# Attention phases of a two-block model on one core: scores, transposes and the latent norm placed elsewhere in the engines' queues

## The chip, the core and the metric

One core of a Trainium2 chip (trn2) runs the whole program in one launch. The metric is the device time of that launch in microseconds, lower is better. Engines are named as in the profile: PE (TensorE), DVE (VectorE), ACT (ScalarE), POOL (GpSimd) and SP (SyncE), which issues the weight loads.

## The reference, cut to what matters

Two blocks run on 256 tokens of width 2048 in fp32: first an even and an odd layer, then a retention layer with an MLP. The change lies in the odd layer:

```python
h = rms_norm(x, norm_w); proj = h @ w_in
c_q, c_kv, k_r, z_c, mq, mz = _split(proj, ODD_SPLITS)        # 768, 512, 64, 2048, 512, 512
q  = (rms_norm(c_q,  mla_q_norm_w)  @ mla_w_uq ).reshape(b_, l_, 16, 128 + 64)
kv = (rms_norm(c_kv, mla_kv_norm_w) @ mla_w_ukv).reshape(b_, l_, 16, 128 + 128)
q_nope, q_rope = q[..., :128], rope(q[..., 128:], positions)
k_nope, v = kv[..., :128], kv[..., 128:]
k_rope = broadcast(rope(k_r[:, :, None, :], positions))       # one rotated key for all heads
y_c = causal_block_attention([q_nope, q_rope], [k_nope, k_rope], v) * silu(z_c)
y_m = memory_attention(mq, mem_n, w_mk, w_mv) * silu(mz)      # 4 heads of 128, 256 memory rows
return x + concatenate([y_c, y_m]) @ w_out
```

## The kernel before, in words

**Panels.** All weight products run as a stream of panels in the order of the table PHASES. A panel is a column of 128 outputs with 4 to 16 weight tiles of 128x128. SP loads it into raw (four slots). ACT rounds it to fp32r (w_hi, L405), DVE takes the rest (w_lo, L744); both are done two panels ahead and in two halves, by the helper split(name, i, j, h) of each engine. PE multiplies each tile twice (L1461: w_hi by the high and low parts, 512 columns; L1464: w_lo by the high part, 256 columns). Two accumulators (pj) alternate: when a panel is done, ACT copies one half of the sum (copy_half, L410), DVE adds the other (evac, L753, or L756 and L758 where it is scaled), and only then may the panel after the next begin. Every engine runs its own queue in order, written out by hand. Semaphores tie them together, so an instruction that waits holds all behind it on its engine.

In ACT's and DVE's queues, split(j, 0) waits until PE has begun the second half of panel j (its buffers are two panels deep), split(j, 1) follows the evacuation of panel j.

**The phases around the change.** "latent" and "latent_tail" (11 panels of 16 tiles) give the latents lraw (4 tiles for c_kv, 6 for c_q) and the shared key krA. Behind them ACT squares all ten tiles at once (L615), PE sums the squares over the partitions with ten matmuls against ones (L1704), ACT takes exp(-0.5 ln v) twice (rsqrt, L414 to L418), DVE refines by a Newton step (L769 to L775), rotates krA (L988 to L1194), and scales and splits the latents into lat (L1199, L1207, hi_lo at L763 and L765).

"memq" (L622, L1212, L1707) runs twice over four panels of 16 tiles: two query heads, two gate columns. After panel 2 PE makes the scores of two heads (L1599), after panel 3 it transposes the probabilities (L1478) and multiplies by the values (L1611). DVE scales one latent tile per panel (normalise_q), and takes softmax_shift and softmax_scale together before it splits and evacuates panel 3. At the end of each pass the gate is applied (L1225, L1228, hi_lo), which counts y_mem.

"mla" (L642, L1238, L1724) runs eight times over eight panels with 6, 6, 6, 8, 4, 4, 16 and 16 tiles: q of two heads, the two heads' rope parts, k of two heads (panel 3 has two outputs of 4 tiles), v of two heads, two gate columns. POOL turns the rope part of q (L376) once panel 2 is evacuated, DVE finishes the rotation (L1266, L1268) in its step for panel 3, between split(3, 0) and split(3, 1). PE makes the scores after panel 4 (L1738, L1739), transposes the values after panels 5 and 6 and the probabilities after panel 6 (L1478), and multiplies them after panel 7 (L1758, L1760).

**POOL's queue.** Between the phases POOL issues a few transfers. After y_mem 8, the end of memq, come the mask (L368) and the first half of x from x_spill (L369); it then waits until x has landed (L370) and only then enters the mla loop with L376:

```python
            pool.wait_ge(S["y_mem"], 8)
            pool.dma_start(mask, mla_mask).then_inc(S["mask_loaded"], 16)
            pool.dma_start(xflat[:, 0:2048], x_spill[:, 0:2048]).then_inc(S["x_loaded"], 16)
            pool.wait_ge(S["x_loaded"], 48)
            ...
                pool.wait_ge(evacuated, outputs("mla", i)(2, 1 + NB))
```

DVE waits for the mask (L1235) ahead of the mla loop.

Of the kernel before, what the change touches and what calls it, by code (L numbers as in the profile page):

```python
# [26 lines left out]
T = 256  # L27
# [4 lines left out]
F32 = mybir.dt.float32  # L32
# [78 lines left out]
def build(nc, streams, w_dt, vecs, consts, mla_mask, ret_tab, ret_decay, pos, x, mem, out):  # L111
    ctx = ExitStack()
    with ctx:
# [80 lines left out]
        def cut(j, n):  # L194
# [21 lines left out]
            angle_ready sin_ready mask_loaded latent_ready latent_squares lat_ready krope_ready  # L216
# [127 lines left out]
        def _(pool):  # L344
# [21 lines left out]
            pool.wait_ge(S["x_spilled"], 32)  # L366
            pool.wait_ge(S["y_mem"], 8)
# [25 lines left out]
        def _(act):  # L393
# [225 lines left out]
            rsqrt(NORM["kv"] + 1, *norm_kv[0:2])  # L619
            rsqrt(NORM["q"] + 1, *norm_q[0:2])  # L620

            def memq_body(i):  # L622
                O = outputs("memq", i)
                M = Count(4, 2, i)
                for j in range(4):
                    if j == 3:
                        mem_exp(M, 2, lambda u: mx[:, u], [p_m[:, 0:512], p_m[:, 512:1024]],
                                [vh_m[:, 0:256], vh_m[:, 256:512]],
                                lambda u: values[:, :, bass.ds(i * 256 + 128 * u, 128)])
                    split("memq", i, j, 0)  # L630
                    copy_half("memq", i, j)
                    if j < 3:
                        split("memq", i, j, 1)
                act.wait_ge(evacuated, O(3, 1 + NB))
                A(mt_m, mz_m, ACT.Tanh, scale=0.5).then_inc(S["mz_tanh"], 1)
                for u in range(2):
                    act.wait_ge(S["mem_pt"], M(u, 1))
                    A(pt_m[:, 512 * u:512 * u + 512], mx[:, 2 + u], ACT.Copy).then_inc(S["mem_pt_copied"], 1)
                split("memq", i, 3, 1)
            act.wait_ge(S["kv_loaded"], 16)  # L640
            run(act, "memq", memq_body)
            def mla_body(i):  # L642
                O = outputs("mla", i)
                for j in range(8):
                    if j == 6:
# [7 lines left out]
                        act.drain().then_inc(S["mla_probs"], 1)  # L653
                    if j == 7:
# [5 lines left out]
                    if j != 3:  # L660
                        split("mla", i, j, 0)
# [72 lines left out]
        def _(dve):  # L734
# [253 lines left out]
            def rope(dst, tmp):  # L988

                for h in range(4):  # L990
                    a, b = 32 * h, 32 * (h ^ 1)
                    TT(tmp[a:a + 32], dst[b:b + 32], sinT[b:b + 32], ALU.mult)
                dve.drain()
                TT(dst, dst, cosT, ALU.mult)
                dve.drain()
                ins = TT(dst, dst, tmp, ALU.add)
                dve.drain()
                return ins

# [187 lines left out]
            variance(NORM["kv"] + 1, 0, 512, norm_kv[0])  # L1187
            variance(NORM["q"] + 1, 1, 768, norm_q[0])

            dve.drain()  # L1190
            rope(krA, rope_t)
            v.tensor_copy(krB[64:128], krA[64:128])
            v.memset(krB[0:64], 0.0)
            dve.drain()  # L1194
            v.memset(krA[64:128], 0.0).then_inc(S["krope_ready"], 1)
            dve.wait_ge(S["rsqrt_ready"], NORM["kv"] + 1)
            newton(*norm_kv)
            for c in range(4):
                STT(out=lraw[:, c], in0=lraw[:, c], scalar=V("kv_norm", c), in1=norm_kv[3], op0=ALU.mult,  # L1199
                    op1=ALU.mult)  # L1200
            hi_lo((lat[:, 0:4, 0], lat[:, 0:4, 1]), lraw[:, 0:4]).then_inc(S["lat_ready"], 1)
            dve.wait_ge(S["rsqrt_ready"], NORM["q"] + 1)
            newton(*norm_q)

            def normalise_q(c):
# [775 lines left out]
```

## Time and profile before

| | |
|---|---|
| median of 3 runs | 2830.67 us (2828.84 to 2835.06) |
| profiled execution | 2829.0 us, its span 2827.5 us |
| PE busy | 2759.5 us, 98% |
| DVE busy | 1956.2 us, 69% |
| ACT busy | 1412.8 us, 50% |
| POOL busy | 35.4 us, 1% |
| L744 (w_lo) | 1010 times, mean 1130 ns |
| L405 (w_hi) | 1010 times, mean 978 ns |
| L1461 / L1464 (hs) | 4400 times each, mean 400 / 280 ns |

All times are on the profile's clock from the start of the span. Matmuls overlap: an L1461 and an L1464 of 400 and 280 ns follow each other so that a pair starts every 0.35 us. memq begins at about 888 us and mla at 960 us; mla ends at about 1208 us.

### The profile page before, as it was taken

The page shows a single profiled execution, that of the slowest core. Times are in us where ns is not written, and L with a number is a line of the kernel's source. Part 1 is how long each engine was busy: PE and PEld are TensorE (multiplying, and loading weights), DVE is VectorE, ACT ScalarE, POOL GpSimd, SP SyncE. Part 2 cuts the span into 40 slices and gives each one's busy share as a digit, 9 for nine tenths or more (in the row PEclk, how much of TensorE's full clock was granted, in tenths as well). Part 3 has the DMA queues.
Part 4 walks back from the last instruction along what each step waited for, and adds up shares of the span by engine and source line. Part 5 has one row for each costly group of instructions (what it writes and reads, how often), then busy time and mean ns, then how long its engine had stood idle before and what let it go on. Part 6 is the DMA issues. An engine that isn't in the chain of part 4 may idle for free.

```text
span 2827.5 us, 46051 instructions
## 1 busy us (share of the span) xinstructions
PE 2759.5 (98%) x15758; PEld 2394.6 (85%) x15758; DVE 1956.2 (69%) x3098; ACT 1412.8 (50%) x2218; POOL 35.4 (1%) x56
## 2 busy tenths in 40 slices
PE   6999999999999899999999999999999999999998
PEld 5888888888888788888888888888888888888887
DVE  5566568878777677777766666666777576675775
ACT  5544345555554555556555544555554444444444
POOL 0000000000000001000000000000000000000000
PEclk9999899999999999999999999999999999999999
DMA  5555354444674334466545555555555555555553
GB/s 231 196 186 185 119 194 157 157 146 144 213 241 162 105 128 159 152 189 200 181 169 177 179 191 186 172 175 171 174 190 185 187 185 187 185 187 185 186 186 112
DMA packets 76349, 495.73 MB, mean 175 GB/s; under 512 B 8544, under 2 KB 8672, under 8 KB 23792
## 3 DMA queue, kind: packets, MB, share of 16 engines
q1 hardware_dynamic: 73568, 478.18, 49.3%
q0 software_dynamic: 2000, 13.70, 1.3%
q10 hardware_dynamic: 704, 2.83, 0.3%
q8 instruction: 47, 0.77, 0.1%
q14 instruction: 30, 0.25, 0.0%
HBM read 486.29 MB, written 8.39 MB: 175 GB/s over the span
## 4 chain that ended last, share of the span: by engine, by line
PE 92%; DVE 3%; ACT 2%; DVEq 2%; issue 1%; DMA 1%; ACTq 0%; POOLq 0%
PE pj L1461 56%; PE pj L1464 28%; PE mx L1478 1%; PE mx L1534 1%; ACT w_hi L405 1%; DVE w_lo L744 1%; PE pj L1570 1%; PE mx L1798 0%; PE mx L1805 0%; DVEq L947 0%; PE mx L1623 0%; PE mx L1738 0%; PE mx L1739 0%; PE mx L1790 0%; PE mx L1611 0%
## 5 line engine op out<-in xcount | busy, mean ns | idle before, releaser
L1461 PE MATMUL pj<-hs,w_hi 128*128 128x512 f32 x4400 | 1564.5, 400 | 4.8 <-DVE xT L758 4.8
L744 DVE TENSOR_TENSOR w_lo<-raw,w_hi 128x1024 fp32r<-128x1024 f32 x1010 | 1136.7, 1130 | 469.3 <-ACT w_hi L405 451.2
L405 ACT ACTIVATE w_hi<-raw 128x1024 fp32r<-128x1024 f32 x1010 | 982.6, 978 | 652.7 <-PE pj L1461 640.2
L1464 PE MATMUL pj<-hs,w_lo 128*128 128x256 f32 x4400 | 1230.1, 280 | 0.0
L1461 PEld LDWEIGHTS pj<-hs,w_hi 128*128 128x128 f32 x4400 | 827.0, 188 | 202.3 <-DVE xT L758 5.1
L1461 PE MATMUL pj<-ys,w_hi 128*128 128x512 f32 x2496 | 885.7, 400 | 8.5 <-DVE ys L809 4.0
L1464 PEld LDWEIGHTS pj<-hs,w_lo 128*128 128x128 f32 x4400 | 830.6, 189 | 3.6 <-issue 2.9
L1464 PE MATMUL pj<-ys,w_lo 128*128 128x256 f32 x2496 | 700.6, 281 | 0.0
L1461 PEld LDWEIGHTS pj<-ys,w_hi 128*128 128x128 f32 x2496 | 471.1, 189 | 126.2 <-DVE ys L809 4.3
L1464 PEld LDWEIGHTS pj<-ys,w_lo 128*128 128x128 f32 x2496 | 473.2, 190 | 0.0
L410 ACT ACTIVATE half<-pj 128x256 f32<-128x256 f32 x491 | 186.6, 380 | 571.8 <-PE pj L1464 559.5
L753 DVE TENSOR_TENSOR gen<-pj,half 128x256 f32<-128x256 f32 x412 | 173.8, 422 | 148.1 <-ACT half L410 146.3
L1461 PE MATMUL pj<-lat,w_hi 128*128 128x512 f32 x272 | 102.3, 415 | 3.9 <-DVE gen L753 2.4
L949 DVE TENSOR_TENSOR xT<-xT,gen 128x256 f32 (+1 forms) x144 | 61.3, 425 | 27.9 <-issue 27.5
L1464 PE MATMUL pj<-lat,w_lo 128*128 128x256 f32 x272 | 76.9, 283 | 0.0
L1461 PEld LDWEIGHTS pj<-lat,w_hi 128*128 128x128 f32 x272 | 51.8, 190 | 20.8 <-issue 4.9
L523 ACT ACTIVATE gen<-xT 128x256 f32 (+1 forms) x64 | 26.8, 418 | 63.6 <-DVE xT L949 63.4
L1464 PEld LDWEIGHTS pj<-lat,w_lo 128*128 128x128 f32 x272 | 52.1, 192 | 0.2
L765 DVE TENSOR_TENSOR ys<-gen,ys 128x256 f32 (+2 forms) x84 | 37.8, 450 | 13.6 <-issue 13.3
L756 DVE TENSOR_TENSOR gen<-pj,half 128x256 f32<-128x256 f32 x59 | 25.0, 423 | 26.2 <-ACT half L410 25.9
L1478 PE MATMUL mx<-con,xT 128*128 128x128 f32 x136 | 21.2, 307 | 20.7 <-DVE xT L802 19.3
L954 DVE TENSOR_TENSOR gen<-gen 128x256 f32<-128x256 f32 x80 | 32.3, 420 | 11.8 <-ACT gen L523 11.8
(279 smaller groups left out, 1411.9 us busy)
## 6 DMA issues: line engine op xcount, KB each, us to landing
raw<-in_w_up SPq DMA_DIRECT2D x64, 1024.0 KB, 4.7
raw<-in_w_down SPq DMA_DIRECT2D x64, 1024.0 KB, 4.8
raw<-in_w_ssd SPq DMA_DIRECT2D x48, 1024.0 KB, 4.7
raw<-in_w_ret_a SPq DMA_DIRECT2D x48, 1024.0 KB, 4.7
raw<-in_w_ret_b SPq DMA_DIRECT2D x48, 1024.0 KB, 4.8
raw<-in_w_out SPq DMA_DIRECT2D x64, 640.0 KB, 3.9
raw<-in_w_gate SPq DMA_DIRECT2D x32, 1024.0 KB, 4.8
raw<-in_w_mem SPq DMA_DIRECT2D x16, 1024.0 KB, 4.9
```

The costliest lines, as they stand in the source:

```text
L405: A(w_hi[:, s, 0:b - a, :], raw[:, c.slot(p, 4), a:b, :], ACT.Copy).then_inc(hi_ready, 1)
L410: A(half[:, c.slot(o, NB)], pj[:, c.slot(o, NB), 0:T], ACT.Copy).then_inc(half_copied, weight)
L744: TT(w_lo[:, s, 0:b - a, :], raw[:, c.slot(p, 4), a:b, :], w_hi[:, s, 0:b - a, :].bitcast(F32), ALU.subtract).then_inc(split_ready, 1)
L753: TT(dst, pj[:, k, T:2 * T], half[:, k], ALU.add).then_inc(evacuated, weight)
L765: return TT(dst[1], src, dst[0].bitcast(F32), ALU.subtract)
L949: TT(xo, xo, res[(o + u) % 2], ALU.add).then_inc(S["x_tile"], 1)
L954: TT(acc[k], acc[k], sq[k][o % 2], ALU.add)
L1461: ins = mm(pj[:, k], w_hi[:, s + h, u], m, start=opens and t == 0, stop=False)
L1464: ins = mm(pj[:, k, 0:T], w_lo[:, s + h, u], m[:, 0], start=False, stop=closes and t == order[-1])
L1478: return nc.tensor.transpose(dst, src, ident)
L1534: ins = mm(mx[:, 0, 32 * r:32 * r + 32], hs[:, k, part, 128 * r:128 * r + 128].bitcast(F32), wdt[:, k], start=k == 0 and part == 0, stop=k ...
L1570: ins = mm(pj[:, k], w_hi[:, s + h, u], src[:, t], start=t == 0, stop=False)
```

## The change

Five edits. PE sums squares over only two tiles (one per norm), after DVE has added the ten tiles to two; these two matmuls stand in the middle of memq's first panel. The memory scores and the transposes of the probabilities move into panels 2 and 3 of memq. memq is written out twice, and the latent scaling is cut in pieces: ACT makes the high part, DVE the low part. The key's rotation goes from DVE to POOL, and the second memory gate goes behind panel 2 of the first mla pass. In mla the scores go from behind panel 4 into panel 6 (before its tile 2), the value transposes into panel 6 (tile 10), the probability transposes into panel 7 (tile 9). DVE and ACT handle the softmax one panel later and after the split of the same step. The mask is waited for in panel 6's step.

```diff
 @@ POOL
             pool.wait_ge(S["x_spilled"], 32)
+            pool.wait_ge(S["krope_in"], 1)
+            for h in range(4):
+                a, b = 32 * h, 32 * (h ^ 1)
+                nc.gpsimd.tensor_tensor(rope_t[a:a + 32], krA[b:b + 32], sinT[b:b + 32], ALU.mult)
+            pool.drain()
+            nc.gpsimd.tensor_tensor(krA, krA, cosT, ALU.mult)
+            pool.drain()
+            nc.gpsimd.tensor_tensor(krA, krA, rope_t, ALU.add)
+            nc.gpsimd.memset(krB[0:64], 0.0)
+            pool.drain()
+            nc.gpsimd.tensor_copy(krB[64:128], krA[64:128])
+            pool.drain()
+            nc.gpsimd.memset(krA[64:128], 0.0).then_inc(S["krope_ready"], 1)
             pool.wait_ge(S["y_mem"], 8)
 @@ ACT, memq (and, per pass, latent_high pieces: wait lat_scaled k, copy to lat[:, c, 0])
-            rsqrt(NORM["kv"] + 1, *norm_kv[0:2])
-            rsqrt(NORM["q"] + 1, *norm_q[0:2])
...
                 for j in range(4):
-                    if j == 3:
+                    split("memq", i, j, 0)
+                    if i == 0 and j == 0:
+                        rsqrt(NORM["kv"] + 1, *norm_kv[0:2])
+                        rsqrt(NORM["q"] + 1, *norm_q[0:2])
+                    if i == 0 and j == 1:
+                        latent_high(1, 4)
+                    if j == 2:
                         mem_exp(...)
...
                     copy_half("memq", i, j)
...
+                    split("memq", i, j, 1)
 @@ ACT, mla
+                for j in range(8):
+                    if j != 3:
+                        split("mla", i, j, 0)
+                    if j == 6:
+                        exps()
                     if j == 7:
                         act.wait_ge(S["mla_vt"], i * 1 + 1)
...
-                    if j != 3:
-                        split("mla", i, j, 0)
 @@ DVE, latent_tail
                 split("latent_tail", 0, j, 0)
+                if j == 2:
+                    dve.wait_ge(S["latent_squares"], 1)
+                    TT(lsq[:, 0:2], lsq[:, 0:2], lsq[:, 2:4], ALU.add)
+                    TT(lsq[:, 4:7], lsq[:, 4:7], lsq[:, 7:10], ALU.add)
+                    dve.drain()
+                    TT(lsq[:, 0], lsq[:, 0], lsq[:, 1], ALU.add)
+                    TT(lsq[:, 4], lsq[:, 4], lsq[:, 5], ALU.add)
+                    dve.drain()
+                    TT(lsq[:, 4], lsq[:, 4], lsq[:, 6], ALU.add).then_inc(S["latent_sums"], 1)
                 evac("latent_tail", 0, j, ...)
                 split("latent_tail", 0, j, 1)
...
-            rope(krA, rope_t)
...
+            dve.drain().then_inc(S["krope_in"], 1)
 @@ DVE, memq (low_latent(k, c): wait lat_hi k, subtract into lat[:, c, 1])
                 for j in range(4):
-                    if j < 3:
-                        normalise_q(i * 3 + (4 + j))
-                    if j == 3:
+                    if j == 2:
                         softmax_shift(M, 2, lambda u: mx[:, u])
+                    split("memq", i, j, 0)
+                    if i == 0 and j == 0:
+                        variance(NORM["kv"] + 1, 0, 512, norm_kv[0])
+                        variance(NORM["q"] + 1, 1, 768, norm_q[0])
+                    if i == 0 and j == 2:
+                        dve.wait_ge(S["krope_ready"], 1)
+                    if j == 2:
                         softmax_scale(M, 2, [p_m[:, 0:512], p_m[:, 512:1024]])
...
                     evac("memq", i, j, ...)
...
+                    split("memq", i, j, 1)
+                    if i == 0 and j == 0:
+                        dve.wait_ge(S["rsqrt_ready"], NORM["q"] + 1)
+                        newton(*norm_q)
+                        newton(*norm_kv[0:3], lnv)
+                        scale_latent(4, "q_norm", lrstd).then_inc(S["lat_scaled"], 1)
...
+                if i == 0:
+                    memq_gate(0)
-            run(dve, "memq", memq_body)
-            dve.wait_ge(S["mask_loaded"], 16)
+            memq_body(0)
+            memq_body(1)
 @@ DVE, mla
-            def mla_body(i):
+            def mla_body(i, opening=False):
                 for j in range(8):
-                    if j == 5:
+                    if j == 6:
+                        dve.wait_ge(S["mask_loaded"], 16)
                         dve.wait_ge(S["mla_scores"], i * 1 + 1)
...
+                    if j != 3:
+                        split("mla", i, j, 0)
                     if j == 6:
                         dve.wait_ge(S["mla_probs"], i * 1 + 1)
...
-                    if j != 3:
-                        split("mla", i, j, 0)
...
                     split("mla", i, j, 1)
+                    if opening and j == 2:
+                        memq_gate(1)
...
-            run(dve, "mla", mla_body)
+            mla_body(0, True)
+            run(dve, "mla", mla_body, 1)
 @@ PE
-            pe.wait_ge(S["latent_squares"], 1)
...
+            def latent_stats():
+                pe.wait_ge(S["latent_sums"], 1)
+                for k, c in ((0, 0), (1, 4)):
+                    mm(mx[:, k, 0:T], ones, lsq[:, c], start=True, stop=True).then_inc(S["stat_ready"], 1)
...
+                def scores():
+                    pe.wait_ge(evacuated, O(1, 1 + NB))
...
+                def probs():
...
+                    whole("memq", i, j, hs,
+                          mid={8: latent_stats} if i == 0 and j == 0 else {5: scores} if j == 2 else
+                          {10: probs} if j == 3 else {})
...
                     panel("mla", i, j, (
...
+                        mid={2: scores, 10: value_rows} if j == 6 else {9: probs} if j == 7 else {})
```

In the diff, `mid={t: f}` runs f on PE's queue before tile t of that panel.

## Rows read from the trace of the kernel before

**Rows 1.** PE's waits over the whole span: who was waited for, total us, times, longest

```profile
PE mx L1738 <- DVEq L1269: 9.2, 8, 1.3
PE mx L1611 <- ACT xT L638: 4.9, 2, 2.5
PE pj L1461 <- DVE xT L758: 4.8, 1, 4.8
...
PE pj L1461 <- DVE gen L753: 3.5, 7, 2.4
```

**Rows 2.** Timeline of PE around the squares' sums: start us, length us, line

```profile
888.39 4.58 PE L1704 MATMUL mx<-xT,con 128*128 128x256 f32 x20
...
908.84 0.80 PE L1461 MATMUL pj<-hs,w_hi 128*128 128x512 f32 x1 [4.77 <-DVE xT L758]
```

**Rows 3.** Stretches: us, PE, PEld, DVE, ACT, POOL busy (instructions), granted clock, DMA

```profile
913.00:914.00 1.00, 1.00 (x6) 0.84 (x5) 1.00 (x2) 0.00 (x0) 0.00 (x0) 0.83 0.95 401
...
968.00:969.00 1.00, 1.00 (x5) 0.80 (x4) 0.76 (x2) 0.99 (x3) 0.00 (x0) 0.50 1.14 418
```

**Rows 4.** Timeline of PE, first value product, first mla panel and its panel 6

```profile
927.36 3.49 PE L1611 MATMUL mx<-xT 128*128 128x256 f32 x8 [2.37 <-ACT xT L638]
...
960.08 0.58 PE L1461 MATMUL pj<-lat,w_hi 128*128 128x512 f32 x1
...
980.18 0.48 PE L1461 MATMUL pj<-hs,w_hi 128*128 128x512 f32 x1
```

**Rows 5.** Timeline of ACT, the two rsqrt

```profile
893.35 0.42 ACT L418 ACTIVATE xT<-xT 128x256 f32<-128x256 f32 x1
893.79 1.28 ACT L414 ACT_TABLE_LOAD   x1
...
896.01 1.28 ACT L405 ACT_TABLE_LOAD   x1
```

**Rows 6.** Timeline of DVE, the split behind the squares and one Newton step

```profile
889.31 1.23 DVE L744 TENSOR_TENSOR w_lo<-raw,w_hi 128x1024 fp32r<-128x1024 f32 x1 [3.45 <-ACT w_hi L405]
...
897.41 0.42 DVE L769 TENSOR_TENSOR xT<-xT 128x256 f32<-128x256 f32 x1
...
899.42 1.67 DVE L1199 SCALAR_TENSOR_TENSOR gen<-gen,vec,xT 128x256 f32<-128x256 f32 x4
```

**Rows 7.** Timeline of DVE, the second memory gate

```profile
960.47 0.69 DVE L1228 SCALAR_TENSOR_TENSOR xT<-mx,xT 128x512 f32<-128x512 f32 x1 [1.85 <-PE mx L1611]
...
961.92 0.69 DVE L765 TENSOR_TENSOR ys<-xT,ys 128x512 f32 x1 [0.17 <-issue]
```

**Rows 8.** Timeline of POOL, the load of x and the first rotation

```profile
963.71 0.53 POOL L369 DMA_DIRECT2D xT<-x_spill  x1
971.45 3.21 POOL L376 TENSOR_TENSOR gen<-gen 32x256 f32<-32x256 f32 x4 [7.21 <-DVE gen L753]
```

**Rows 9.** DMA issues from 955 to 1010 us: KB each, median us to landing

```profile
xT<-x_spill POOLq DMA_DIRECT2D x1, 1024.0 KB, 5.9
```

**Rows 10.** Timeline of PE in the second mla pass, panel 4 to panel 6

```profile
1004.83 0.28 PE L1464 MATMUL pj<-lat,w_lo 128*128 128x256 f32 x1
1006.40 0.49 PE L1738 MATMUL mx<-gen 128*128 128x128 f32 x2 [1.29 <-DVEq L1269]
...
1009.47 0.40 PE L1461 MATMUL pj<-lat,w_hi 128*128 128x512 f32 x1
...
1010.67 0.48 PE L1461 MATMUL pj<-hs,w_hi 128*128 128x512 f32 x1
```

**Rows 11.** Timeline of DVE in the same pass

```profile
1004.52 0.96 DVE L744 TENSOR_TENSOR w_lo<-raw,w_hi 128x256 fp32r<-128x256 f32 x1
...
1006.52 1.56 DVE L744 TENSOR_TENSOR w_lo<-raw,w_hi 128x256 fp32r<-128x256 f32 x2 [0.20 <-issue]
1008.00 0.42 DVE L753 TENSOR_TENSOR gen<-pj,half 128x256 f32<-128x256 f32 x1
...
1014.61 1.01 DVE L1257 TENSOR_SCALAR xT<-xT,small 128x128 f32<-128x128 f32 x4
```

More of the change, by code:

```diff
@@ L629, in memq_body, with exps @@
                                 lambda u: values[:, :, bass.ds(i * 256 + 128 * u, 128)])
-                    split("memq", i, j, 0)
+                    if j == 3:
+                        for u in range(2):
+                            act.wait_ge(S["mem_pt"], M(u, 1))
+                            A(pt_m[:, 512 * u:512 * u + 512], mx[:, 2 + u], ACT.Copy).then_inc(S["mem_pt_copied"], 1)
                     copy_half("memq", i, j)
-                    if j < 3:
[L633 to L639, printed above, removed]
+                    if j == 3:
+                        act.wait_ge(evacuated, O(3, 1 + NB))
+                        A(mt_m, mz_m, ACT.Tanh, scale=0.5).then_inc(S["mz_tanh"], 1)
+                    split("memq", i, j, 1)
+                    if i == 0 and j == 2:
+                        latent_high(2, 5)
+                        latent_high(3, 6)
+                    if i == 0 and j == 3:
+                        latent_high(4, 7)
+                    if i == 1 and j == 0:
+                        latent_high(5, 8)
+                        latent_high(6, 9)
+                    if i == 1 and j == 2:
+                        latent_high(7, 0, 4)
             act.wait_ge(S["kv_loaded"], 16)
-            run(act, "memq", memq_body)
+            memq_body(0)
+            memq_body(1)
             def mla_body(i):
                 O = outputs("mla", i)
-                for j in range(8):
-                    if j == 6:
+                def exps():
                         act.wait_ge(S["mla_shift"], i * 1 + 1)
@@ L1196, in _ @@
[L1196 to L1205, printed above, removed]
-                STT(out=lraw[:, c], in0=lraw[:, c], scalar=vec[:, bass.ds(c + VEC["kv_norm"][0], 1)],
-                    in1=lrstd, op0=ALU.mult, op1=ALU.mult)
-                yy = lat[:, c]
-                hi_lo((yy[:, 0], yy[:, 1]), lraw[:, c]).then_inc(S["lat_ready"], 1)
+            dve.drain().then_inc(S["krope_in"], 1)
@@ new lines, in memq_body @@
+                    if i == 0 and j == 3:
+                        low_latent(2, 5)
+                        low_latent(3, 6)
+                        scale_latent(7, "q_norm", lrstd).then_inc(S["lat_scaled"], 1)
+                    if i == 1 and j == 0:
+                        low_latent(4, 7)
+                    if i == 1 and j == 1:
+                        low_latent(5, 8)
+                        low_latent(6, 9)
+                    if i == 1 and j == 3:
+                        low_latent(7, 0, 4)
@@ new lines, in memq_body @@
+                    if i == 1 and j == 0:
+                        for c in (8, 9):
+                            scale_latent(c, "q_norm", lrstd).then_inc(S["lat_scaled"], 1)
+                    if i == 1 and j == 1:
+                        for c in range(4):
+                            ins = scale_latent(c, "kv_norm", lnv)
+                        ins.then_inc(S["lat_scaled"], 1)
+                if i == 0:
+                    memq_gate(0)
+            memq_body(0)
+            memq_body(1)
```

122 lines of the change are left out of this document (54 added, 68 removed).

## The prediction

> **What bounds it now.** I began with the page: PE is busy 98% of the span, so a gain can only be a wait of PE, a matmul left out, or a stretch at the lower clock. The second view is the list of PE's waits. In these phases they are few: 9.2 us before the mla scores, once in each of the 8 passes, 4.9 before the memory values (two), 4.8 before memq's panel 2 and, within the 3.5 of the last row, one of 2.4 before mla's panel 2, where DVE sits out the mask's load [rows 1]. The third view is PE's timeline: the ten matmuls on the squares are 20 instructions in 4.58 us, 0.23 each, and nothing runs beside them [rows 2]. The fourth is the granted clock: behind a long wait it falls to 0.50, which is 1.2 GHz: the tile at 908.84 takes 0.80 us instead of 0.40 [rows 2], the clock is back at 2.4 GHz from about 913.4, and it is 0.50 again at 968 [rows 3]. The first value product took 3.49 us for 8 instructions, where 8 times 0.23 is 1.83 [rows 2, 4]; so such a stretch costs about 1.7 us, and the one behind the wait of 4.77 us, from 908.8 to 913.4, about 2.3 (half of 4.6). The fifth view is DVE's timeline inside an mla pass, because DVE releases every panel.
>
> **Part 1, squares.** 16 of the 20 instructions go: -3.7 us [rows 2]. The two left wait for DVE's sums. DVE issues the split at 889.3 and is free 1.14 us later, at 890.45 [rows 6]; the adds follow: 0.69 and about 0.95 for 512 and 768 columns, three of 0.42 and the drains (0.42 for 256 columns, 0.69 for 512 [rows 6, 7]; 768 extrapolated), 2.9 in all: 893.35. PE reaches tile 8 of memq's panel 0 at about 891.0. A wait of 2.4 us is new; before it was 0.25.
>
> **Part 2, memq's norm chain.** PE goes on at 893.4, spends 0.9, is at tile 8 at 894.3 and ends panel 0 at 897.1 (8 tiles of 0.35). ACT's split for panel 2 needs that tile 8, and both rsqrt now stand behind it: split 894.8 to 895.9, table load 1.28, Ln and Exp, load, Ln and Exp, a third load [rows 5]: about 902.05. Only then comes copy_half of panel 0, and DVE's evacuation at 903.3. Panel 2 needs it: PE is done with panel 1 at 902.65 and waits 0.7. Then DVE has in one row: split 1.14, two Newton steps of 2.0 [rows 6], a scaling 0.5, split 1.14, and the evacuation of panel 1, 0.85: 903.5 + 7.6 = 911.1. PE wants that one before tile 5 of panel 2, for the scores, at 905.1: a wait of 6.0. So the 4.8 of [rows 1] does not go; the chain of tables and Newton steps is as long as before and takes its place. In memq's second pass the gate of the first, two splits and five small operations on DVE make a wait of 1.6 at the same tile. The transposes inside panel 3 do remove the two waits before the values: six tiles (2.1 us) now cover ACT's copies. Waits in memq: before 0.25 + 4.8 + 4.9 = 10.0; after 2.4 + 0.7 + 6.0 + 1.6 = 10.7. Clock: before 2.3 + 1.7, after 2.3. Sum of parts 1 and 2: -3.7 + 0.7 - 1.7 = **-4.7**; mla begins at 955.4 instead of 960.1 [rows 4].
>
> **The key's rotation on POOL** is free for PE if it ends before DVE's softmax_scale, over 15 us later. The nearest price is 3.21 us for four operations on 32 partitions [rows 8]: seven to ten such, and by partitions up to 14 us. Its harm is to DVE: beside POOL's rotation a split of 256 columns took 0.96 us, where the two in [rows 11] share 1.56 with one of four times the size. I take 0 and keep 0 to 2 us. The Trainium skill, SBUF — State Buffer, section "Who interferes with whom", says that a DVE instruction with two SBUF inputs and a GpSimd one that reads SBUF lock each other out for a whole instruction; by that rule the split ahead of the variances is held by one POOL operation and the sum gains 0.8.
>
> **Part 3, first mla pass.** This is the dear one. The second gate moves behind panel 2. It ends in y_mem 8, and behind y_mem 8 in POOL's queue stand the mask, the load of x, the wait until x has landed, and only then the rotation of q. Count from M, the pass's first tile. Panels 0 to 2 (18 tiles of 0.353) end at M+6.4; DVE splits, evacuates panel 2 at 7.7, splits until 8.1. The gate is an operation of 0.77, then 2.14 from L1228 to the end of L765 [rows 7]: M+11.0. POOL issues the load of x 1.1 later (962.61 to 963.71, [rows 7, 8]), it lands 5.9 after issue [rows 9]: M+18.0. Rotation 3.2 [rows 8], DVE's part 0.9 and gap, then the split that panel 5's second half waits for: M+22.9. Split of panel 6 (1.14) and evacuation of panel 4 (0.4): panel 6 begins at M+24.5. Its 34 tiles ahead are 12.0, so 12.5 us are waits, 2.2 of them before panel 4 (its output waits behind the gate) and 9.5 inside panel 5. Behind 9.5 us without work the clock is low as in [rows 3]: I take 1.6. Before, panel 6 came at M+20.1 [rows 4]: 12.0 for tiles, 2.9 for scores and transposes, 5.1 waits and clock. Pass 1: 12.5 + 1.6 - 5.1 = **+9.0**. The mask's own wait of 2.4, in that 5.1, is hidden now; the load of x is not.
>
> **Part 4, the seven other passes.** The scores leave the place between panels 4 and 5, and with them the 1.29 us wait for DVE's L1269. But they were the cover for DVE. Its order up to the second split of panel 6 is unchanged: the first split of panel 5 ends at 1005.48, the rotation follows, the second split of panel 5 ends at 1006.93, that of panel 6 at 1008.08, and the evacuation of panel 4, which panel 6 must have, at 1008.42 [rows 11]. PE is done with panel 4 at 1004.95. Now it waits 0.6 for the first, works 0.7, waits 0.8 for the second, works 0.7, waits 0.8 for the third: panel 6 begins at 1008.47. Before it began at 1010.67 [rows 10], with 2.72 for scores (1006.40 to 1009.47 less a tile) and 0.22 for two transposes ahead of it, which move behind. 1008.47 + 2.94 - 1010.67 = +0.74 a pass, times seven: **+5.2**. Behind that nothing waits: scores end 3.4 after panel 6's start, the softmax needed 6.5 from 1009.1 to 1015.6 [rows 11], is put behind a split on either engine (1.3), and is wanted 8.4 after the scores; the copies for the value product keep about 0.6 us of cover. If that cover is gone, each pass pays what is missing, up to the 1.1 us of one ACT split.
>
> **Sum.** -4.7 + 9.0 + 5.2 = +9.5 us on the profiled 2829.0, that is 2838.5. The median of the runs is 1.7 higher, and I give the time on its basis: **2840.2**. Bounds of the parts: 1 and 2 from -8 (no third table load, a shorter chain) to -1 (POOL in DVE's way, a low clock behind the 2.4 us wait too); 3 from +5 (x lands in 3 us, clock holds) to +11; 4 from +4 to +9. The likeliest case's own range is 2835 to 2846. 0.2% is 5.7 us and about what a measurement of this kernel can tell from no change; so 2825.0 and 2836.3 are the borders.
>
> **Rivals.**
> Waits gone (faster, 0.12): the mla scores come out of DVE's way and panels 5 and 6 find their weights ready. It would need DVE's steps at 1006.5 and 1008.0 to come earlier; they depend on the evacuations of panels 3 and 4 and on POOL, which the change leaves. The place is panel 6's start; it decides if DVE is ready within 1.1 us of panel 4's end, not 3.5. Each pass then saves 1.3 to 1.45, 10 for seven; with -4.7 and +9.0, 2824.8. Against it speak [rows 11].
> Load of x hidden (0.20): POOL's wait ends early, because x lands sooner or the gate comes sooner, and pass 1 costs 0 to +2. Then -4.7 + 1 + 5.2: 2832. For it: a mean of 5.9 for a single transfer is one sample; against it, even a load of 2.6 us would leave 6 of waits.
> Clock falls in the loop (0.10): in 3.5 us after panel 4 PE works only 1.4, in seven passes. Each fall costs 1.7, so +12 on the sum: 2852. Against it: behind the wait of 1.29 us the tiles take 0.40 us, the length at full clock [rows 10]. The Trainium skill, TensorE: Matmul & The Clock Gate, section "A second HAM failure mode: psum-queue depth-cycling", says that short idles between groups can make the clock swing; no row here shows it for gaps this short.
> Nothing moves (0.03): the edit acts only where PE was idle anyway; 2830.7.
> Forecast, parts as worked: 0.55.
>
> **Chances.** Slower by over 0.2%: 0.50 of the forecast's 0.55, the clock's 0.10, a little of the load's: 0.62. Within 0.2%: 0.26. Faster: 0.12. The range 2827 to 2850 leaves out the fast rival, and the clock rival's far end.
>
> **What the profile of after should show.** PE's waits: the row for the mla scores gone; in its place about 0.6, 0.8 and 0.8 us at L1461 in panels 5 and 6, eight times, released by DVE's L744 and L753; an mla pass 0.7 to 0.8 us longer. In pass 1 a single wait near 9.5 us inside panel 5 and POOL's L376 (its new line) beginning about 7 us behind DVE's last step of the gate. In memq a wait of 6 us before the scores, no wait before the values, four instructions on the squares instead of 20. If mla passes are shorter than before, part 4 is wrong; if mla's pass 1 is not at least 5 us longer, part 3 is; if memq's first scores do not wait, part 2.

## The result, and the profile after

The changed kernel takes 2836.88 us (median of 20 runs, 2828.88 to 2840.64), the kernel before on the same chips 2828.71 (20 runs, 2822.80 to 2835.06): a ratio of 1.003, 95% interval 1.0023 to 1.0038, so 8.2 us slower. Forecast were 2840.2 and slower; the range 2827 to 2850 holds it. The profiled execution took 2840.31 us, its span 2838.8.

**PE's waits**, the whole span: engine, line waited for, total us, times, longest.

```profile
PE pj L1514 <- DVE w_lo L778: 16.1, 16, 9.1
PE pj L1514 <- DVE gen L787: 6.9, 15, 1.5
PE mx L1652 <- DVE xT L792: 5.9, 2, 5.0
...
PE mx L1758 <- DVE xT L1215: 2.1, 1, 2.1
```

The row for the mla scores [rows 1] is gone, and so is the one for the memory values. In their place stand DVE's splits (L778) with 16.1 us, of which 9.1 are a single wait, and its evacuations (L787). The timeline of PE shows where:

```profile
894.21 2.05 PE L1758 MATMUL mx<-xT,con 128*128 128x256 f32 x4 [2.06 <-DVE xT L1215]
...
912.11 3.78 PE L1652 MATMUL mx<-kv,xT 128*128 128x256 f32 x8 [5.02 <-DVE xT L792]
...
942.92 1.99 PE L1652 MATMUL mx<-kv,xT 128*128 128x256 f32 x8 [0.87 <-DVE xT L792]
...
956.53 0.58 PE L1514 MATMUL pj<-lat,w_hi 128*128 128x512 f32 x1
...
967.66 0.50 PE L1514 MATMUL pj<-lat,w_hi 128*128 128x512 f32 x1 [1.49 <-DVE gen L787]
...
979.17 0.79 PE L1514 MATMUL pj<-lat,w_hi 128*128 128x512 f32 x1 [9.12 <-DVE w_lo L778]
...
1009.89 0.49 PE L1514 MATMUL pj<-lat,w_hi 128*128 128x512 f32 x1 [0.42 <-DVE w_lo L778]
1011.28 0.49 PE L1514 MATMUL pj<-lat,w_hi 128*128 128x512 f32 x1 [0.43 <-DVE w_lo L778]
1012.75 0.50 PE L1514 MATMUL pj<-hs,w_hi 128*128 128x512 f32 x1 [0.51 <-DVE gen L787]
```

In this order they are: the four instructions of the sums; the memory scores of both passes; mla's first tile; in pass 1 panel 4 and the second half of panel 5; in pass 2 the three small waits, in panel 5 (twice) and at panel 6, that come back in each later pass.

**Why the 9.1.** DVE's and POOL's timelines in pass 1:

```profile
966.58 0.69 DVE L799 TENSOR_TENSOR ys<-xT,ys 128x512 fp32r<-128x512 f32 x1
...
977.64 0.42 DVE L1316 TENSOR_TENSOR gen<-gen 128x256 f32<-128x256 f32 x1 [9.37 <-POOL gen L389]
```

```profile
967.57 0.60 POOL L381 DMA_DIRECT2D xT<-in_mla_mask  x1 [63.73 <-DVE ys L799]
968.17 0.54 POOL L382 DMA_DIRECT2D xT<-x_spill  x1
974.57 3.04 POOL L389 TENSOR_TENSOR gen<-gen 32x256 f32<-32x256 f32 x4 [5.86 <-DMA xT<-x_spill]
```

The gate ends at 967.3, POOL issues mask and x, waits 5.86 us for x and turns q only then. DVE stands for 9.37 us with the split of panel 5 queued behind the wait.

**The granted clock** in stretches (us, PE, PEld, DVE, ACT, POOL busy, clock, DMA):

```profile
894.00:900.00 6.00, 5.79 (x23) 4.94 (x24) 4.07 (x7) 2.37 (x3) 3.60 (x4) 0.72 0.46 153
...
912.00:914.00 2.00, 1.89 (x5) 1.53 (x6) 2.00 (x5) 0.00 (x0) 0.00 (x0) 0.50 0.00 0
914.00:916.00 2.00, 2.00 (x6) 1.64 (x5) 1.16 (x4) 0.00 (x0) 0.00 (x0) 0.50 0.84 221
916.00:918.00 2.00, 2.00 (x7) 1.65 (x7) 0.79 (x2) 0.00 (x0) 0.00 (x0) 0.51 0.72 303
...
1338.00:1341.00 3.00, 3.00 (x11) 2.52 (x11) 0.84 (x3) 0.41 (x2) 0.00 (x0) 0.50 0.22 90
```

The clock is at 1.2 GHz behind the wait of 2.06 us (until about 897.5), behind that of 5.02 (until 918) and behind the 9.12. The last row lies outside the change, behind a wait of 1.26 us in a later layer norm; the kernel before has the same 1.26 us there, and its profiled run stayed at 2.4 GHz. It is in no part of the change and costs this one execution about 2 us.

**The balance** of the two profiled runs, by three marks: ACT's squares (885.99 before, 886.71 after), mla's first tile, the starts of the passes.

| stretch | before | after | difference | forecast |
|---|---|---|---|---|
| squares to mla's first tile | 74.09 | 69.82 | -4.3 | -4.7 |
| mla pass 1 | 33.81 | 41.87 | +8.1 | +9.0 |
| passes 2 to 8, each | 30.56 | 31.25 | +0.69, seven times +4.8 | +0.74, +5.2 |
| sum | 321.80 | 330.41 | +8.6 | +9.5 |

The rest of the two runs' difference of 11.3 us is 0.7 ahead of the squares and the 2 us of the clock at 1338.

### The profile page after: what moved, and what is told of

It is laid out like the page before. It is cut to its first block, busy times and chain, and to the rows that moved or that the text cites. A ratio compares the mean times of both kernels' runs of the same rounds, so it can differ in the third digit from the quotient of the medians.

```text
span 2838.8 us, 45848 instructions
## 1 busy us (share of the span) xinstructions
PE 2763.5 (97%) x15742; PEld 2393.7 (84%) x15742; DVE 1953.4 (69%) x3087; ACT 1414.3 (50%) x2224; POOL 41.6 (1%) x65
## 4 chain that ended last, share of the span: by engine, by line
PE 91%; DVE 4%; ACT 2%; DVEq 1%; issue 1%; DMA 1%; POOL 0%; ACTq 0%; POOLq 0%
PE pj L1514 56%; PE pj L1517 28%; PE mx L1531 1%; DVE w_lo L778 1%; ACT w_hi L418 1%; PE mx L1587 1%; PE pj L1623 1%; PE mx L1860 0%; PE mx L1867 0%; DVEq L981 0%; PE mx L1676 0%; PE mx L1792 0%; PE mx L1793 0%; PE mx L1852 0%; PE mx L1652 0%
## 5 line engine op out<-in xcount | busy, mean ns | idle before, releaser
L778 DVE TENSOR_TENSOR w_lo<-raw,w_hi 128x1024 fp32r<-128x1024 f32 x1010 | 1136.7, 1131 | 473.2 <-ACT w_hi L418 457.0
L787 DVE TENSOR_TENSOR gen<-pj,half 128x256 f32<-128x256 f32 x412 | 173.8, 422 | 145.3 <-ACT half L423 142.8
L799 DVE TENSOR_TENSOR ys<-gen,ys 128x256 f32 (+3 forms) x84 | 37.8, 451 | 14.2 <-issue 13.9
L790 DVE TENSOR_TENSOR gen<-pj,half 128x256 f32<-128x256 f32 x59 | 24.9, 422 | 30.7 <-ACT half L423 30.6
```

Source lines behind the costliest of these rows:

```text
L778: TT(w_lo[:, s, 0:b - a, :], raw[:, c.slot(p, 4), a:b, :], w_hi[:, s, 0:b - a, :].bitcast(F32), ALU.subtract).then_inc(split_ready, 1)
L787: TT(dst, pj[:, k, T:2 * T], half[:, k], ALU.add).then_inc(evacuated, weight)
L799: return TT(dst[1], src, dst[0].bitcast(F32), ALU.subtract)
```

## The experiments

All of them in one table first: the ratio to the kernel before of the same session, and three lengths from each one's trace (us).

| kernel | median | ratio (95% interval) | squares to mla | pass 1 | passes 2 to 8 |
|---|---|---|---|---|---|
| before | 2828.71 | 1 | 74.09 | 33.81 | 30.56 |
| changed | 2836.88 | 1.0030 (1.0023 to 1.0038) | 69.82 | 41.87 | 31.25 |
| 1 rotation first | 2825.29 | 0.999 (0.9981 to 0.9999) | 67.12 | 33.11 | 31.23 |
| 2 scores back | 2829.39 | 1.0001 (0.9992 to 1.001) | 68.03 | 42.15 | 30.47 |
| 3 rotation's end later | 2826.79 | 1.000 (0.9991 to 1.0009) | 68.81 | 40.19 | 30.64 |
| 4 ten sums | 2834.38 | 1.002 (1.0011 to 1.003) | 68.68 | 43.54 | 31.23 |
| 5 Newton later | 2831.50 | 1.0016 (1.0007 to 1.0025) | 63.82 | 41.54 | 31.21 |
| 6 = 1 + 3 | 2821.25 | 0.998 (0.997 to 0.9989) | 69.84 | 34.24 | 30.72 |
| 7 key on DVE | 2836.72 | 1.0032 (1.0019 to 1.0045) | 70.88 | 41.73 | 31.32 |
| 8 = 1 + 3 + 5 | 2818.26 | 0.9964 (0.9954 to 0.9974) | 63.14 | 33.40 | 30.69 |
| 9 = 1 + 2 + 5 | 2817.51 | 0.9965 (0.9951 to 0.9979) | 63.21 | 33.07 | 30.50 |
| 10 = 9, sums later | 2812.85 | 0.995 (0.9936 to 0.9963) | 62.88 | 33.34 | 30.48 |
| 11 gate back | 2829.73 | 1.0008 (0.9999 to 1.0017) | 68.77 | 37.40 | 31.21 |
| 12 = 10 + 11 | 2811.95 | 0.995 (0.9937 to 0.9963) | 62.89 | 33.44 | 30.52 |

A length in one trace holds falls of the clock of 1.5 to 3 us each, which come and go between runs of one kernel (last section); differences of 1 to 2 us in the first two lengths are not a kernel's.

**1. POOL turns q of pass 1 before it waits for the gate, the mask and x.**

```diff
-            pool.wait_ge(S["y_mem"], 8)
-            pool.dma_start(mask, mla_mask).then_inc(S["mask_loaded"], 16)
-            pool.dma_start(xflat[:, 0:2048], x_spill[:, 0:2048]).then_inc(S["x_loaded"], 16)
-            pool.wait_ge(S["x_loaded"], 48)
...
-            run(pool, "mla", mla_body)
+            mla_body(0)
+            pool.wait_ge(S["y_mem"], 8)
+            pool.dma_start(mask, mla_mask).then_inc(S["mask_loaded"], 16)
+            pool.dma_start(xflat[:, 0:2048], x_spill[:, 0:2048]).then_inc(S["x_loaded"], 16)
+            pool.wait_ge(S["x_loaded"], 48)
+            run(pool, "mla", mla_body, 1)
```

> The changed kernel, but POOL turns q of the first mla pass before it waits for the gate, loads the mask and loads x. My theory (the first pass stands still for the landing of x in POOL's queue): the wait of 9.1 us inside panel 5 shrinks to the 0.4 us of the other passes and no low clock follows, the first pass shrinks from 41.9 to 32 to 33 us, the whole is 9 us shorter than the changed kernel (about even with the kernel before, or 0 to 2 us faster). Rival (the second memory gate in DVE's queue makes the first pass long): the pass stays above 38 us, because DVE is late in any case, and the whole is at most 3 us shorter.

PE's timeline, panels 4 and 6 of pass 1:

```profile
961.22 0.50 PE L1515 MATMUL pj<-lat,w_hi 128*128 128x512 f32 x1 [2.76 <-DVE gen L788]
965.16 0.50 PE L1515 MATMUL pj<-hs,w_hi 128*128 128x512 f32 x1 [0.90 <-DVE gen L788]
```

The wait of 9.12 is gone, pass 1 is 8.8 us shorter, passes 2 to 8 are as they were. So the loss of pass 1 is POOL's queue. What is left before panel 4 (2.76) is the gate itself, made longer by POOL, which now works beside it: its first operation takes 1.23 us, in the changed kernel 0.68, and the whole gate 4.0 instead of 2.7. The medians differ by 11.6 us, more than pass 1 explains; what the rest is stays open.

**2. mla's scores and transposes, and DVE's and ACT's steps for them, where the kernel before has them.**

```diff
-                        mid={2: scores, 10: value_rows} if j == 6 else {9: probs} if j == 7 else {})
+                    if j == 4:
+                        scores()
+                    if j in (5, 6):
+                        value_rows(j - 5)
+                    if j == 6:
+                        probs()
...
```

On DVE and ACT the softmax steps go back one panel, and split(j, 0) stands behind them again.

> The changed kernel with PE, ACT and DVE of the mla loop in the order of before (scores behind panel 4, softmax a panel earlier), all else as changed. My theory (the scores covered DVE's splits of panels 5 and 6): passes 2 to 8 go back from 31.25 to 30.55 us, the three waits of 0.4 to 0.5 us become one of 1.2 to 1.3, the whole is 4.9 to 6 us shorter than the changed kernel. Rival (the passes are longer for another reason, the order of exp and copies on ACT or POOL beside DVE): they stay within 0.2 us of 31.25.

```profile
PE mx L1790 <- DVEq L1317: 18.3, 8, 9.8
```

Passes 2 to 8 go back to 30.47, pass 1 stays at 42: the 0.7 us a pass come from mla's part of the change. The run takes that part back whole, PE's scores and transposes with DVE's and ACT's order, so it does not tell these apart; experiment 3 does, for DVE. The 9.8 us now stand at the scores of pass 1.

**3. DVE evacuates panel 4 and splits panels 5 and 6 before it finishes q's rotation.**

```diff
                         split("mla", i, j, 0)
-                        dve.wait_ge(S["rope_turned"], i * 1 + 1)
-                        TT(qr, qr, cosT, ALU.mult)
-                        dve.drain()
-                        TT(qr, qr, qro, ALU.add)
-                        dve.drain().then_inc(S["qk_ready"], 1)
...
+                    elif j == 4:
+                        evac("mla", i, 5, vtm[0])
+                        split("mla", i, j, 0)
...
+                    if j == 4:
+                        dve.wait_ge(S["rope_turned"], i * 1 + 1)
+                        TT(qr, qr, cosT, ALU.mult)
+                        dve.drain()
+                        TT(qr, qr, qro, ALU.add)
+                        dve.drain().then_inc(S["qk_ready"], 1)
```

> The changed kernel, but DVE evacuates panel 4 and makes the second half of panel 5 and the first half of panel 6 before it finishes the rotation of q, which the scores in panel 6 now leave time for. My theory (DVE's order, not its amount of work, sets the start of panel 6): the waits before panel 5's second half and panel 6 go, one of at most 0.5 us before the scores may come, each of passes 2 to 8 is 0.7 to 1.1 us shorter (30.2 to 30.5), the first pass 2 to 3 us shorter; 7 to 10 us in all. Rival (DVE is simply full in this stretch): the wait moves to the scores, and the pass stays above 31.

Each later pass loses only 0.08 against before (30.64), with the scores and ACT's order where the change puts them: 0.61 of the 0.69 us were DVE's order. The theory's 30.2 to 30.5 are missed all the same, and pass 1 gives 1.7 us, not 2 to 3, because 5.83 us turn up at its scores. The three waits become two, 0.42 and 0.53 us in pass 2: the splits are ahead of the rotation, but fall beside POOL's products, which hold the first of them; two of 256 columns take 1.29 us, where 0.42 each is usual (pass 3):

```profile
1034.62 1.29 DVE L778 TENSOR_TENSOR w_lo<-raw,w_hi 128x256 fp32r<-128x256 f32 x2
```

That fits the first wait. Ahead of the second, DVE also waits 0.24 us for ACT's copy of panel 4, so POOL as its only cause is not shown.

**4. No sums on DVE; the ten matmuls on the squares, at the changed place.**

```diff
-                    TT(lsq[:, 0:2], lsq[:, 0:2], lsq[:, 2:4], ALU.add)
...
-                for k, c in ((0, 0), (1, 4)):
-                    mm(mx[:, k, 0:T], ones, lsq[:, c], start=True, stop=True)
+                for k, (a, b) in enumerate(((0, 4), (4, 10))):
+                    for c in range(a, b):
+                        ins = mm(mx[:, k, 0:T], ones, lsq[:, c], start=c == a, stop=c == b - 1)
...
```

> The changed kernel without DVE's adds: PE sums the ten squared tiles with ten matmuls, at the same place before tile 8 of memq's first panel. My theory (the norm chain through ACT and DVE sets the start of the memory scores, so matmuls left out on PE buy little): no wait before the sums, 4.6 us of sums, no low clock there, the scores' wait about as long as now, and mla's first tile within 1 us of the changed kernel's. Rival (the 3.7 us of matmuls were worth their price): mla starts 2.5 to 3.7 us later.

```profile
885.82 4.48 PE L1753 MATMUL mx<-xT,con 128*128 128x256 f32 x20
```

PE works 4.48 us on the sums again, and yet the stretch is no longer than the changed kernel's, 68.68 against 69.82; the intervals of the two ratios overlap. (Pass 1 is 1.7 us longer in this trace, with a wait of 9.62 and a longer stretch at 1.2 GHz, and no line of the edit acts there.) DVE's sums save PE 16 instructions and hand back a wait of 2.06 us, in that run also the clock. On their own they are worth nothing that can be measured.

**5. In memq's first pass DVE evacuates panel 1 before the two Newton steps.**

```diff
-                    if i == 0 and j == 0:
+                    if i == 0 and j == 1:
                         dve.wait_ge(S["rsqrt_ready"], NORM["q"] + 1)
                         newton(*norm_q)
                         newton(*norm_kv[0:3], lnv)
                         scale_latent(4, "q_norm", lrstd).then_inc(S["lat_scaled"], 1)
```

(ACT's latent_high(1, 4) goes behind its split of panel 1.)

> The changed kernel, with one order altered in memq's first pass: DVE evacuates panel 1 before it does the two Newton steps, ACT's copy of the first latent tile goes behind its split of panel 1. Theory (the 5.0 us before the memory scores are DVE's order, not its amount of work): that wait goes; what stays is at most a wait of 2 to 3 us later in the phase, since DVE has the same work to do and PE is no longer waiting while it does it. From the start of the squares to mla's first tile 65 to 68 us instead of the changed kernel's 69.8; the rest as the changed kernel, so 2 to 5 us less than it in all. Rival (DVE as such is the bound of this pass): the wait moves whole to the next panel, 69 to 71 us, no gain.

```profile
900.72 1.90 PE L1651 MATMUL mx<-kv,xT 128*128 128x256 f32 x8
...
910.71 1.43 PE L1530 MATMUL mx<-con,xT 128*128 128x128 f32 x8 [0.67 <-DVE xT L1018]
...
930.53 1.99 PE L1651 MATMUL mx<-kv,xT 128*128 128x256 f32 x8 [1.48 <-DVE xT L792]
```

The first scores wait for nothing; 0.67 us turns up at the transposes of the probabilities and the second pass waits 1.48 instead of 0.87. The stretch is 6.0 us shorter: 3.4 of waits (2.06 + 5.02 + 0.87 in the changed kernel, 2.43 + 0.67 + 1.48 now) and 2.8 of clock. At 63.8 us it is shorter than the theory's 65 to 68. The order was the bound, not DVE's amount of work.

**7. The key's rotation on DVE again.** (6 and 8 are taken together below.)

```diff
-            pool.wait_ge(S["krope_in"], 1)
...
-            dve.drain().then_inc(S["krope_in"], 1)
+            dve.drain()
+            for h in range(4):
+                a, b = 32 * h, 32 * (h ^ 1)
+                TT(rope_t[a:a + 32], krA[b:b + 32], sinT[b:b + 32], ALU.mult)
...
```

On DVE the rotation stands behind its last split of latent_tail.

> The changed kernel with the key's rotation back on DVE, behind its last split of latent_tail, as it stood before; POOL has no part in memq. Theory (moving it to POOL was worth what DVE would need for it, about 3 to 4 us in its busiest stretch, less the 0.5 us that POOL's presence costs a split): the wait before the memory scores grows from 5.0 to 7 to 9 us, squares to mla 72 to 74 us, 2 to 4 us more than the changed kernel in all. Rival (DVE has slack there, or waits for ACT's rsqrt anyway, and POOL's reads of SBUF slow it): the wait stays at 5 us or shrinks, no difference or up to 1 us less.

The theory failed: 70.88 us, 1.1 more, and 1.0032 beside 1.0030. The changed kernel's DVE stands idle for 1.86 and for 3.13 us in this stretch:

```profile
897.89 1.72 DVE L778 TENSOR_TENSOR w_lo<-raw,w_hi 128x1024 fp32r<-128x1024 f32 x1 [1.86 <-ACT w_hi L418]
...
903.39 0.42 DVE L790 TENSOR_TENSOR xT<-pj,half 128x256 f32<-128x256 f32 x1 [3.13 <-ACT half L423]
```

That takes most of the rotation; 0.93 us of a new wait, before a panel, is what shows on PE.

**6 and 8. The edits together.** 6 is 1 and 3; 8 adds 5.

> The changed kernel with two of the earlier edits together: POOL rotates q of the first mla pass before it waits for y_mem 8 and x, and DVE evacuates panel 4 and does its split for panels 5 and 6 before it finishes the rotation. Theory (the loss of the change is these two waits, and they are independent): pass 1 takes 32 to 34 us, passes 2 to 8 30.6 each, so 8.5 + 4.5 = 13 us less than the changed kernel, 0.995 to 0.996 of it; against the kernel before 0.997 to 0.999. Rival (the two overlap: with the rotation finished later the scores, or DVE beside POOL, hold the pass): passes 2 to 8 stay near 31.2 and the time is that of the first edit alone, 0.999 of the kernel before.

> The changed kernel with all three edits that its waits suggest: POOL's rotation first, DVE's rotation later in each mla pass, Newton steps behind the evacuation of memq's panel 1. Theory (the change's idea is sound and its loss is in three places of the order): squares to mla 65 to 68 us, pass 1 32 to 34, passes 2 to 8 30.6; 0.994 to 0.995 of the changed kernel, 0.996 to 0.998 of the kernel before. Rival (what is taken out at one place comes back at the next one, since DVE is the engine behind all three): no better than the kernel with the first two edits, or within 0.2% of the kernel before.

They add up: pass 1 at 34.2 and 33.4, the later ones at 30.7, and with edit 5 the stretch before mla at 63.1. 8 is 18.6 us below the changed kernel in median (2836.88 less 2818.26) and 0.9964 of the one before. Its trace shows no fall of the clock from the squares to the end of pass 1; 6 has three there, and one kernel's next execution may have more or fewer (last section).

**9. As 8, but mla in the order of before (2) in place of 3.**

> The kernel with three edits (rotation first, DVE's rotation later, Newton steps later), but with mla's scores and transposes back where the kernel before has them, and with DVE's and ACT's order of before in mla. Theory (mla's part of the change is worth nothing, the gain of the kernel with three edits over the one before is all memq's and pass 1's): passes 2 to 8 take 30.5 us as in the run with mla's part undone, 0.25 each less than with the three edits, so 0 to 2 us less than it in all; pass 1 32 to 34 us; 0.995 to 0.997 of the kernel before. Rival (the moved scores are what fills pass 1 while the gate holds DVE): pass 1 grows by 1 us or more and the time is 1 us or more above the kernel with three edits.

0.9965 beside 0.9964, passes at 30.50 instead of 30.69: mla's part of the change is worth nothing that can be measured, even mended. Of the 12.0 us by which its trace is shorter than before from the squares to the end of pass 8, 10.9 are memq's (74.09 to 63.21). No run divides these between the fewer matmuls, the moved transposes and the cut scaling.

**10. As 9, sums at tile 14 of memq's panel 0 instead of tile 8.**

```diff
-                          mid={8: latent_stats} if i == 0 and j == 0 else ...
+                          mid={14: latent_stats} if i == 0 and j == 0 else ...
```

> As the run before it, with one number altered: PE's two matmuls on the summed squares stand before tile 14 of memq's panel 0 instead of tile 8. Theory (the wait of 2.4 us there only says that PE comes too early for DVE's sums; DVE's sums end where they end, and six tiles are 2.1 us): the wait falls to 0.3 to 0.5 us, and since ACT's rsqrt begins later by nothing (it waited for the same sums), squares to mla is 1.5 to 2.5 us shorter. Rival (ACT's split for panel 2, which waits for tile 8, now comes 2 us earlier than the rsqrt and changes nothing, but the evacuation of panel 0 stands behind the rsqrt, so PE waits there instead): the wait moves to panel 2's first tile, 1 to 2 us, no gain.

```profile
893.17 1.13 PE L1756 MATMUL mx<-xT,con 128*128 128x256 f32 x4 [0.25 <-DVE xT L1214]
...
901.39 0.47 PE L1512 MATMUL pj<-hs,w_hi 128*128 128x512 f32 x1 [0.73 <-DVE xT L791]
...
905.15 1.99 PE L1650 MATMUL mx<-kv,xT 128*128 128x256 f32 x8 [1.78 <-DVE xT L791]
```

In the trace the rival is right: the wait of 2.06 falls to 0.25, and 0.73 before panel 2 and 1.0 more at the scores (0.75 in run 9) take its place; the stretch is 0.3 us shorter. The median is 4.7 lower than run 9's, but over five runs each the intervals overlap, and the trace does not show such a gain. Kernel 12 below has the later sums too and stands at the same 0.995, against 0.9964 and 0.9965 for 8 and 9, so a gain is likely, though not shown. One source would be invisible in these traces: 8 and 9 were profiled in executions in which the clock held behind the sums' wait, which other kernels with that wait did not always manage (last section).

**11 and 12. The second memory gate back at the end of memq**, in the changed kernel and in kernel 10.

```diff
-                if i == 0:
-                    memq_gate(0)
+                memq_gate(i)
...
-                    if opening and j == 2:
-                        memq_gate(1)
```

> The changed kernel with the second memory gate back at the end of memq's second pass; POOL's queue stays as in the changed kernel. Theory (the gate's place behind panel 2, by what stands behind y_mem 8 in POOL's queue, is the cause of the 9.1 us wait): the gate ends 6 us earlier, about 5 us behind mla's first tile, x lands at 12, the rotation is through at 16; so the wait inside panel 5 is 4 to 5 us and the one of 1.5 before panel 4 goes. Pass 1 takes 36 to 38 us instead of 41.9; about 4 to 6 us less than the changed kernel. Rival (the load of x would be late wherever the gate stands, or DVE's gate holds a split at the start of the phase): pass 1 stays above 40 us.

> The kernel with the late sums (rotation first, mla's order of before, Newton steps later, sums before tile 14), with the second memory gate back at the end of memq's second pass too. Theory (the 2.8 us before panel 4 are the gate, in front of the evacuation of panel 2; at the end of memq PE's panels have 16 tiles, so DVE has more time there): that wait goes, pass 1 takes 30.5 to 31.5 us instead of 33.3; 1 to 3 us less in all, 0.994 to 0.995 of the kernel before. Rival (DVE's 2.9 us are owed in either place): a wait of 1 to 3 us turns up before one of mla's panels 1 to 3 instead, no gain.

```profile
960.73 0.47 PE L1511 MATMUL pj<-lat,w_hi 128*128 128x512 f32 x1 [1.88 <-DVE gen L787]
...
971.50 0.80 PE L1511 MATMUL pj<-lat,w_hi 128*128 128x512 f32 x1 [2.63 <-DVE w_lo L778]
```

In 11 (the rows) the gate ends 5.5 us behind mla's first tile (at 959.8, the tile at 954.3) instead of 10.7, and pass 1 takes 37.40, inside the 36 to 38 of the theory; the wait in panel 5 is 2.63 in place of 9.12 (4 to 5 were expected), and 1.88 before panel 2 is new (none was). So both halves made the 9.1: the gate's place, and what POOL queues behind it. In 12 the theory failed. 2.77 us before panel 4 became 1.95 before panel 2 and 0.96 at the scores of pass 1, in all 2.91; 33.44 against 33.34. DVE's gate, 2.7 us of work, is owed in either place.

## Why the prediction was right, point by point

**The time.** The sum was +9.5 us on the profiled run. The three stretches give +8.6, the medians +8.2 (interval of the ratio: +6.5 to +10.7). The predicted 2840.2 is 3.3 above the median; 2.0 of that is its base (2830.67 from three runs, 2828.71 from twenty), 1.3 the sum.

**Part 1, squares.** Right in its times: adds from 891.17 to 894.06, 2.9 us, and a wait of 2.06 for 2.4. Too kind in its sum: it booked -3.7 in full, and experiment 4 shows that with the ten matmuls back nothing is lost. The term that failed is the clock: "Clock: before 2.3 + 1.7, after 2.3". It fell behind the 2.06 too and stayed low for 5.9 us behind the 5.02, 4.5 in all.

**Part 2, memq's chain.** The central claim held: the 4.8 of [rows 1] did not go, DVE's chain of tables and Newton steps took its place with 5.02 at the scores (6.0 was said), and the waits for the values vanished. Two steps failed. "A third load": ACT's timeline shows two and goes straight to copy_half:

```profile
897.87 1.28 ACT L427 ACT_TABLE_LOAD   x1
...
900.89 1.28 ACT L427 ACT_TABLE_LOAD   x1
...
902.99 0.37 ACT L423 ACTIVATE half<-pj 128x256 f32<-128x256 f32 x1
```

so panel 2 did not wait 0.7. Why the copy behind the second pair needed no load here, where the kernel before has one at L405 [rows 5], no run shows. And the second pass waited 0.87, not 1.6. Waits 7.95 for 10.7, clock 4.5 for 2.3: 12.5 for 13.0. That -4.7 met -4.3 is luck: two errors that cancel.

What the prediction left unasked is whether the chain could lie elsewhere. It took the 6.0 as the price of the norm; experiment 5 shows that one step of DVE's order holds it, and that the change in memq was then worth 11 us, waits and clock together (74.1 to 63.2, run 9).

**The key's rotation.** Taken at 0, and 0 it is (experiment 7). POOL's rows:

```profile
896.23 3.96 POOL L370 TENSOR_TENSOR xT<-gen 32x256 f32<-32x256 f32 x4 [65.17 <-DVEq L1218]
897.78 0.74 POOL L370 TENSOR_TENSOR xT<-gen 32x256 f32<-32x256 f32 x1
898.58 1.61 POOL L370 TENSOR_TENSOR xT<-gen 32x256 f32<-32x256 f32 x1
...
901.01 0.74 POOL L372 TENSOR_TENSOR gen<-gen 128x256 f32<-128x256 f32 x1 [0.82 <-issue]
```

The first row is all four products of L370; the next two are the third and the fourth of them by themselves.

The bound "by partitions up to 14 us" was far off: an operation on 128 partitions costs 0.74, no more than one on 32. Its harm to DVE is in the row of experiment 7: a split of 1.72 us instead of 1.22. It begins at 897.89, 0.1 us into POOL's third product, and ends at 899.61, 1.1 us behind that product's end at 898.52; the fourth product, begun at 898.58, ends at 900.19, 0.6 behind the split. So first the split stood for POOL and then POOL for the split: 0.5 us on DVE, some 0.9 on POOL. The Trainium skill's rule (SBUF — State Buffer, "Who interferes with whom"), that the two engines lock each other out, agrees with these rows. The 0.8 that the prediction worked out by it was 0.3 too much, since one operation is held for what is left of the other's, not for all of it.

**Part 3, pass 1.** From M = 956.53: the gate ended at M+10.7 (M+11.0 said), the load was issued 0.9 later, the rotation began at M+18.0 (M+18.0 said), panel 5 went on at M+22.6 (M+22.9), panel 6 began at M+24.1 (M+24.5). Waits 1.49 and 9.12 for 2.2 and 9.5, clock 1.8 for 1.6. +8.1 for +9.0, and experiments 1 and 11 tie it to POOL's queue and to the gate's place.

**Part 4, the other passes.** +0.69 for +0.74, at the three places named. Panel 6 of pass 2 begins 14.35 us into the pass, where 14.58 was worked out. The waits shown are 0.42, 0.43 and 0.51 where 0.6, 0.8 and 0.8 were said, but the rows name only a part of each gap: from the first to the second are 1.39 us, of which 0.43 are listed as idle and two tiles are 0.70. Experiment 2 puts the 0.7 on mla's part of the change, experiment 3 puts 0.61 of it on the order of DVE, which the scores had covered.

**The rivals.** "Waits gone" needed DVE's steps to come earlier, and the change leaves them; experiment 3 moved them and found the same passes as before, not the 1.3 us shorter ones that this rival priced, since two waits stay. "Load of x hidden" and "Nothing moves": no. "Clock falls in the loop": no; from 990 to 1220 us the mean granted clock of the changed kernel is 1.00, with three gaps in each pass. The Trainium skill's rule on short idles (TensorE: Matmul & The Clock Gate, "A second HAM failure mode: psum-queue depth-cycling") does not show at gaps of 0.4 to 0.5 us.

## What to carry to other kernels

Where PE waits for a hand-ordered engine, ask first which step of that engine's queue is ahead of the one PE wants, not how much work the engine has: moving one evacuation ahead of two Newton steps was worth more than every matmul saved. Before moving the event that a queue waits for, read what stands behind that wait on the queue: a transfer and a rotation stood behind the gate, and 2.7 us of DVE work put three panels later cost 8. Work placed in the middle of a panel covers the next engine's latency only if its own inputs are early; taking it out from between two panels uncovers whatever it was covering.

## What was not expected of the hardware

The clock's falls are not a function of the wait alone. The wait before the sums is nearly the same in ten of these kernels. Behind 2.04 to 2.44 us the clock fell to 0.50 in five (the changed kernel and runs 2, 5, 6, 7) and stayed at 1.00 in the five others (1, 3, 8, 9, 11), with the same panels ahead of it; 2.06 us is on both sides. Before panel 4 the same holds for 2.76 to 2.82 us (three of five). Behind the waits of 3.88 us and more in these stretches it always fell. Each fall cost 1.4 to 3.0 us. Shorter waits are not safe either: behind 1.72 to 1.81 us near 710 us, ahead of every edit, it fell in 5 of the 14 traces, behind the layer norm's 1.26 to 1.35 us near 1330 in 8 of 14, behind 1.89 us in run 7 and 1.95 us in run 12, but not behind 1.88 us in run 11. So a wait of 1.3 to 3 us carries a second price of about 1.7 in about half of the executions, and one profiled run is a poor witness for less than 3 us.

A small operation on POOL costs the same 0.74 us for 32 and for 128 partitions of 256 elements. POOL and DVE hold one another up by what is left of the instruction that runs: beside POOL a split of 1.22 took 1.72, one of 0.42 took 0.91, an operation of 0.69 took 1.23, and a product of POOL's took 1.61 behind such a split.
